# Delta-rule loop with a 128x4x64 state: carried, query and update products as alternating 64-wide tiles

## What is computed

```python
def gated_delta_rule_chunked(q, k, v, g, beta):
    """S_t = a_t (I - b_t k_t k_t^T) S_{t-1} + b_t k_t v_t^T, o_t = S_t^T q_t. Chunked WY form."""
...
    def step(state, inp):
        u_i, w_i, q_i, k_i, a_i, gl = inp
        v_new = u_i - jnp.einsum("bhid,bhde->bhie", w_i, state)
        o_i = jnp.einsum("bhid,bhde->bhie", q_i, state) + jnp.einsum("bhij,bhje->bhie", a_i, v_new)
        state = state * gl[..., None, None] + jnp.einsum("bhid,bhie->bhde", k_i, v_new)
        return state, o_i
```

## Time and profile before

| | |
|---|---|
| median of 3 runs | 2689.47 us (2685.22 to 2690.39) |
| span of the profiled execution | 2685.3 us |
| granted TensorE clock, mean of the span | 0.985 |
| TensorE busy | 2583.9 us, 96% |
| VectorE, ScalarE, GpSimd busy | 1817.1, 926.3, 549.2 us |

### The profile page before, as it was taken

One profiled execution on the slowest core, in us unless ns is written; L12 is line 12 of the kernel. 1 busy time (PEld: TensorE's weight loads), 2 busy tenths in 40 slices (PEclk: granted clock), 3 DMA queues, 4 the chain that ended last, 5 costly groups with the idle time before them and its releaser, 6 DMA issues. The chain is left out here.

```text
span 2685.3 us, 35832 instructions
## 1 busy us (share of the span) xinstructions
PE 2583.9 (96%) x14026; PEld 2060.8 (77%) x14026; DVE 1817.1 (68%) x2735; ACT 926.3 (34%) x1610; POOL 549.2 (20%) x265
## 2 busy tenths in 40 slices
PE   7999999999899999999999999999999999999998
PEld 5875558884478887788888888867997888887787
DVE  5894997772667668999773553333277666666987
ACT  4335454420444545333332222232233223232432
POOL 1212544430000004333201222134400000003330
PEclk9999999999999999999999999999999999999999
DMA  4011032230133336333221222243413222225231
GB/s 162 32 64 67 32 126 96 90 133 24 55 114 118 103 118 223 111 110 126 91 82 53 78 70 75 81 166 108 145 55 88 79 87 79 87 79 214 100 126 63
DMA packets 192759, 262.24 MB, mean 98 GB/s; under 512 B 15952, under 2 KB 121808, under 8 KB 192208
## 3 DMA queue, kind: packets, MB, share of 16 engines
q1 hardware_dynamic: 192592, 259.95, 28.6%
HBM read 196.80 MB, written 61.93 MB: 96 GB/s over the span
## 5 line engine op out<-in xcount | busy, mean ns | idle before, releaser
L1381 PE MATMUL ps<-gl_t,gl_slot 128*128 128x512 f32 x1056 | 244.6, 391 | 2.4 <-DVE gl_t L3986 2.4
L1389 PE MATMUL ps<-b_hi,a_hi 128*128 128x512 f32 x592 | 231.6, 391 | 9.5 <-DVE sb L3630 7.6
L1381 PEld LDWEIGHTS ps<-gl_t,gl_slot 128*128 128x128 f32 x1056 | 199.3, 189 | 44.6 <-DVE gl_t L3986 3.1
L2756 POOL TENSOR_TENSOR s_raw<-ff_raw 128x1024 f32<-128x1024 f32 x2 | 5.1, 2545 | 962.6 <-DMA ff_raw<-hid_rows 513.6
L3630 DVE TENSOR_TENSOR sb<-sb,ps 128x512 f32<-128x512 f32 x272 | 173.5, 680 | 33.3 <-PE ps L1389 33.2
L1381 PE MATMUL ps<-gl_b,gl_slot 128*128 128x512 f32 x768 | 182.1, 395 | 3.7 <-DVE gl_slot L4018 3.7
L1381 PE MATMUL ps<-ff_t,slot 128*128 128x512 f32 x768 | 179.2, 393 | 4.4 <-DVE ff_t L3284 4.4
L1381 PE MATMUL ps<-H_hi,tw_hi 128*128 128x512 f32 x448 | 175.6, 392 | 0.0
L1381 PE MATMUL ps<-H_rest,tw_hi 128*128 128x512 f32 x448 | 174.4, 389 | 0.0
L1381 PE MATMUL ps<-H_hi,tw_lo 128*128 128x512 f32 x448 | 174.3, 389 | 0.0
L1381 PEld LDWEIGHTS ps<-gl_b,gl_slot 128*128 128x128 f32 x768 | 146.4, 191 | 35.1 <-DVE gl_slot L4018 2.4
(11 more groups left out here) (475 smaller groups left out, 6053.9 us busy)
## 6 DMA issues: line engine op xcount, KB each, us to landing
wraw<-in_w_ff SPq DMA_DIRECT2D x16, 1024.0 KB, 5.9
ff_raw<-ff_rows SPq DMA_DIRECT2D x8, 2048.0 KB, 7.9
slab_raw<-in_w_ff SPq DMA_DIRECT2D x16, 1024.0 KB, 5.1
ff_rows<-quad SPq DMA_DIRECT2D x61, 256.0 KB, 2.0
traw<-in_w_in SPq DMA_DIRECT2D x28, 512.0 KB, 4.3
wq_raw<-in_w_in SPq DMA_DIRECT2D x6, 2048.0 KB, 8.5
wraw<-in_w_gate SPq DMA_DIRECT2D x22, 512.0 KB, 3.9
wraw<-in_w_up SPq DMA_DIRECT2D x22, 512.0 KB, 5.1
```

The lines of the kernel that those rows point to most:

```text
L1381: mm = nc.tensor.matmul(out_ap, stationary(a, k), moving(c, k), start=(k == 0 and n == 0), stop=(k == kts - 1 and n == 2))
L1389: mm = nc.tensor.matmul(out_ap, stationary(a, k), moving(c, k), start=(fresh and k == 0 and n == 0), stop=(k == 1 and n == 2), skip_group_ ...
L2756: G.tensor_tensor(s1, s3, a22, ALU.add).then_inc(dn_as, 1)
```

## The change

The state is kept compact, 128 partitions by 4 by 64: head 2q in the upper 64 partitions, head 2q+1 in the lower. Keys times state becomes, per direction, 8 products with 64 rows of contraction, 128 output rows and 64 columns, alternating between the two halves of the partitions and between two banks. The query-times-state products are made the same way and now stand as one group per direction ahead of that direction's scores-times-values products. The update becomes 8 products of 64 output rows and 64 columns per direction, alternating between the two halves of the output partitions. `forward` alternates between the directions product by product. The keys are decayed ahead of time on GpSimd (a new product of decay and keys into `KdT`, in `decayed_queries`), so VectorE's multiplication by the decay in `less_carried` goes away. The results of the heads of one parity lie in one bank and are taken away with a stride.

```diff
-            order += [("kS", i, d) for d in both] + behind(0, 1)
-            order += pair("y", 0) + behind(2) + pair("w", 1) + behind(3)
+            order += [("kS", i, d, x) for d in both for x in both] + behind(0, 1)
+            order += pair("y", 0) + behind(2, 3) + pair("w", 1)
...
-        Sbd = [[area(gd + 1024 * b + 512 * d, 4, P) for d in range(2)] for b in range(2)]
+        Sc = [[area(gd + 512 * b + 256 * d, 4, HD) for d in range(2)] for b in range(2)]
+        KdT = [area(gd + 1024 + 512 * d, 4, P) for d in range(2)]
...
                 for q in range(4):
-                    mm = nc.tensor.matmul(ps[:, b, q * P:(q + 1) * P], pair_tile(KTall, q, d, i), Sbd[d][i % 2][:, q, :],
-                                          start=True, stop=True)
+                    for x in both:
+                        mm = nc.tensor.matmul(ps[:, banks[x], q * HD:(q + 1) * HD], half(KdT[d], 2 * q + x),
+                                              half(Sc[d][i % 2], 2 * q + x), start=True, stop=True)
...
                 for h in range(HEADS):
+                    for d in both:
+                        rows = block_rows(d, s)
+                        mm = nc.tensor.matmul(ps[rows, banks[d], h * HD:(h + 1) * HD], Gm[i % 2][d][:, h, rows],
+                                              yv[i % 2][d][:, h * HD:(h + 1) * HD], start=True, stop=True)
+                        if h == HEADS - 1:
+                            mm.then_inc(full[banks[d]], 1)
...
+                    for x in both:
+                        cols = slice((2 * q + x) * HD, (2 * q + x + 1) * HD)
+                        mm = nc.tensor.matmul(ps[x * HD:(x + 1) * HD, b, q * HD:(q + 1) * HD], Kdec[d][:, cols],
+                                              yv[i % 2][d][:, cols], start=True, stop=True)
...
+            def carried_outputs(i, d):
...
+                pe.wait_ge(gdn_qd, 2 * i + d + 1)
+                for q in range(4):
+                    for x in both:
+                        nc.tensor.matmul(ps[:, banks[x], q * HD:(q + 1) * HD], half(QdT[(i + 2) % 3][d], 2 * q + x),
+                                         half(Sc[d][i % 2], 2 * q + x), start=(q == 0), stop=False, skip_group_check=True)
+
+            def own_outputs(i, d, x):
...
+                for q in range(4):
+                    h = 2 * q + x
+                    mm = nc.tensor.matmul(ps[:, b, q * HD:(q + 1) * HD], ATm[i % 2][d][:, h, :],
+                                          yv[i % 2][d][:, h * HD:(h + 1) * HD], start=(i == 0),
+                                          stop=(i == 0 or q == 3), skip_group_check=True)
+                mm.then_inc(full[b], 1)
...
+                else:
+                    carried_outputs(i - 1, 1)
+                    own_outputs(i - 1, 1, 0)
+                forward(i, 1)
+                if i > 0:
+                    own_outputs(i - 1, 1, 1)
...
+                    if i > 1:
+                        for x in both:
+                            wait_full(pool, G_GDN, GDN_AT[("kS", i - 1, d, x)])
+                    if i > 0:
+                        G.tensor_tensor(KdT[d], QdT[(i + 2) % 3][d], KTall[:, :, t * P:(t + 1) * P], ALU.mult
+                                        ).then_inc(gdn_keys, 1)
+                        pool.wait_ge(gdn_keys, 2 * (i - 1) + d + 1)
...
-                    V.tensor_tensor(heads_of(Xw[d], HD), heads_of(ps[:, b, :], HD),
-                                    args[:, ECUM, at:at + HEADS].unsqueeze(2).broadcast_to([P, HEADS, HD]), ALU.mult
-                                    ).then_inc(drained[b], 1)
-                for d in both:
-                    ready("kS", i, d)
-                    V.tensor_tensor(Xw[d], KVt[i % 2][d][:, GW:2 * GW], Xw[d], ALU.subtract).then_inc(gdn_X, 1)
+                    for x in both:
+                        b = arrived("kS", i, d, x)
+                        V.tensor_tensor(heads_of(Xw[d], HD)[:, x::2, :], heads_of(KVt[i % 2][d][:, GW:2 * GW], HD)[:, x::2, :],
+                                        heads_of(ps[:, b, 0:256], HD), ALU.subtract).then_inc(drained[b], 1)
...
-                V.tensor_tensor(Sbd[d][(i + 1) % 2], Sbd[d][i % 2],
-                                eglP[:, at, :].unsqueeze(2).broadcast_to([P, 4, P]), ALU.mult).then_inc(gdn_ss, 1)
+                V.tensor_tensor(Sc[d][(i + 1) % 2], Sc[d][i % 2],
+                                eglP[:, at, :].unsqueeze(2).broadcast_to([P, 4, HD]), ALU.mult).then_inc(gdn_ss, 1)
...
-            for d in both:
-                ins = V.memset(Sbd[d][1].rearrange("p a b -> p (a b)"), 0.0)
-            ins.then_inc(gdn_S0, 1)
```

More of the change, by code:

```diff
@@ L1006, in front, with rest_taken @@
             return 0, FRONT_AT[key]
+        def rest_taken(eng, i):
+            for d in range(2):
+                for x in range(2):
+                    wait_drained(eng, G_GDN, GDN_AT[("kS", i, d, x)])
         slab_last = [front("dense", 3, 1), front("dense", 7, 1), front("dense", 11, 1), front("SV", 7)]
@@ L1607, in solve, with forward @@
                             mm.then_inc(full[banks[d]], 1)
[L1609 to L1616, removed]
-                for h in range(HEADS):
-                    mm = nc.tensor.matmul(ps[rows, b, h * HD:(h + 1) * HD], Gm[i % 2][d][:, h, rows],
-                                          yv[i % 2][d][:, h * HD:(h + 1) * HD], start=True, stop=True)
-                mm.then_inc(full[b], 1)
+            def forward(i, s):
+                banks = []
+                for d in both:
+                    if s == 1:
+                        for x in both:
+                            ready("kk", i, d, x)
+                    ready("y", i, d, s - 1)
+                    banks.append(bank("w", i, d, s))
+                for h in range(HEADS):
+                    for d in both:
+                        rows = block_rows(d, s)
[3 more added lines that the diff above has]
+                            mm.then_inc(full[banks[d]], 1)
             def update(i, d):
@@ L1630, in update @@
                 mm.then_inc(full[b], 1)
[L1632 to L1649, removed]
+            def carried_outputs(i, d):
+                banks = [bank("o", i, 2 * d + x) for x in both]
+                if i == 0:
+                    return
+                pe.wait_ge(gdn_qd, 2 * i + d + 1)
[3 more added lines that the diff above has]
+                                         half(Sc[d][i % 2], 2 * q + x), start=(q == 0), stop=False, skip_group_check=True)
@@ new lines, in own_outputs @@
+            def own_outputs(i, d, x):
+                ready("y", i, d, 3)
+                ready("kq", i, d, x)
+                b = where(G_GDN, GDN_AT[("o", i, 2 * d + x)])[0]
+                for q in range(4):
[4 more added lines that the diff above has]
+                mm.then_inc(full[b], 1)
@@ L1673, in _ @@
                     scores("kk", i + 1, 0)
-                for d in both:
-                    forward(i, d, 2)
+                forward(i, 2)
                 if more:
@@ L1680, in _ @@
                     scores("kk", i + 1, 1)
-                for d in both:
-                    forward(i, d, 3)
+                forward(i, 3)
                 if more:
@@ L1688, in _ @@
                         update(i, d)
-            outputs(NT - 1, 0, 1, 2, 3)
+            for d in both:
+                carried_outputs(NT - 1, d)
+                for x in both:
+                    own_outputs(NT - 1, d, x)
             def mix_product(t, h, b, ks):
@@ L3089, in state_add @@
                         dve.wait_ge(gdn_ss, 2 * (i - 1) + d + 1)
-                    for x in both:
-                        part = slice(HD * x, HD * x + HD)
-                        dst = Sbd[d][(i + 1) % 2][part, :, part]
-                        new = heads_of(ps[part, b, :], P)[:, :, part]
-                        ins = V.tensor_tensor(dst, dst, new, ALU.add) if i > 0 else V.tensor_copy(dst, new)
+                    dst, new = Sc[d][(i + 1) % 2], heads_of(ps[:, b, 0:256], HD)
+                    ins = V.tensor_tensor(dst, dst, new, ALU.add) if i > 0 else V.tensor_copy(dst, new)
                     ins.then_inc(drained[b], 1)
@@ L3149, in _ @@
             dve.wait_ge(c_out, 32)
-            for d in both:
-                ins = V.memset(Sbd[d][1].rearrange("p a b -> p (a b)"), 0.0)
-            ins.then_inc(gdn_S0, 1)
-            dve.wait_ge(gdn_S0, 1)
             for t in range(1, NT, 2):
```

55 lines of the change are left out of this document (26 added, 29 removed).

## The result

The changed kernel takes 2722.77 us (median of 4 runs, 2719.57 to 2730.84) against 2688.44 us for the kernel before beside it (4 runs, 2685.22 to 2690.39). The ratio is 1.0132, with a 95% interval of 1.012 to 1.0145: some 34 to 35 us slower. The forecast was 2688.4, no change. In the profiles the span went from 2685.3 to 2729.0 us, and the mean granted TensorE clock from 0.985 to 0.964. The profiled execution of the changed kernel is the longest of its four (2730.84 us); the other three have a mean granted clock of 0.967 to 0.969 and are 7 to 11 us shorter, so the account that follows is for some 8 us more than the median.

What follows compares the result with a forecast made beforehand. TensorE bounds most of an iteration, VectorE's chain the two 5.25 us stretches. -2.4 - 6 x 0.5 + 5 x 0.6 + 0.3 + 1.0 = -1.1 us, giving 2688.4 us, no change; own range 2684 to 2694, stated range 2680 to 2702.

Steps and rivals of the forecast that it cites:

- Carried products cost the same at half the width: Keys times state in the head: twice as many products of half the width take 1.84 us against 1.89.
- Update 1.4, between 0.93 and 1.87: State update in column halves: 1.4 us against 2.07 before, the middle between two bounds.
- The head: Stretch from update to first solve, 6.68 us, set by TensorE; to gain 0.5 us, ends 0.8 and 0.0.
- Forward 1.0, and nothing won by it in the 5.25 us stretches: Interleaved forward takes 1.0 us, not 1.71; second to third and third to fourth solve gain 0, VectorE's subtraction starting later.
- First to second solve 6.3, for the lock: First state_decay meets GpSimd's running product, both reading SBUF: +0.6 us on 5.69, ends +0.3 and +0.9.
- GpSimd's lock costs more: Rival, chance 0.07: second state_decay delays the drain by 1.0 too, +0.9 at the first; +6.5 over the forecast, 2695.
- Iterations 0 and 1 gain 2.4: Start of the loop: first forward of iteration 1 starts 2.1 us earlier, 2.4 with shorter forward; ends 1.0 and 3.4.
- Last outputs +1.0: Final outputs, 9.67 us at half clock: about +1.0 for half-tile records and shape changes, ends 0.5 and 3.
- From span to time: Profile's span of 2684.2 us turned into a measured time by adding 4.2 us: 2688.4.
- column groups do not overlap: Rival, chance 0.07: forward stays 1.71 us, 1.8 us more an iteration over six; +12, 2701.
- the clock falls in the loop: Rival, chance 0.08: gaps of 1 us in the 5.25 us stretches halve TensorE's clock; +17, 2706.

Runs made afterwards that it cites:

- gaps filled: Changed kernel with 4 products of no use, 0.85 us, ahead of every second, third and fourth solve, written into a free bank and overwritten: 2688.34 us, ratio 0.9999.
- forward apart: Changed kernel with the forward products as before, eight of direction 0, then eight of direction 1: 2688.59 us, ratio 0.9985.
- the update whole: Changed kernel with the update as four full 128x128 products per direction as before, the state still compact: 2704.3 us, ratio 1.0044.
- spare products: Products whose results are overwritten, where TensorE idles; in the kernel before, added in iterations 0, 1 and 7: 2690.37 us, ratio 1.0003.

## Why the prediction was wrong

Its costing of a full-clock iteration held:

- *Carried products cost the same at half the width*: 1.83 us for a forecast 1.84.
- *Update 1.4, between 0.93 and 1.87*: 1.20. The head took 5.95 us, a gain of 0.73 for a forecast 0.5, inside the bounds.
- *Forward 1.0, and nothing won by it in the 5.25 us stretches*: 1.02, and 498.82 - 493.57 = 5.25. The chain through VectorE's weighting and subtraction is the bound there, with forward at 1.02 as at 1.71.
- *First to second solve 6.3, for the lock*: 6.23, with the decay at 1.01 us. The second `state_decay` (0.72 us) ended at 494.52, ahead of the drain at 494.70, so the rival *GpSimd's lock costs more* is out.
- *Iterations 0 and 1 gain 2.4*: 0.8. The forward product of iteration 1 started at 429.80 against 429.64, in a loop that began 2.3 us later: 2.1 us gained up to there, as forecast. But from there TensorE ran on at half clock until past 437 us (rows below), and output, solve and scores gave back most of the gain. This term was mis-sized by the clock too.
- *Last outputs +1.0*: 643.52 - 632.65 = 10.87 us for 9.67, +1.2, at half clock before and after.
- *From span to time*: the forecast put 4.2 us between them. Every run on record has its time 1.7 to 2.1 us above its span, so some 2 of the 4.2 were scatter of the profiled execution.
- The rival *column groups do not overlap* is out: forward, whose pairs share all rows, took 1.02 us for 1.71, and the update 1.20 for 32 records, where 32 records of forward one after the other took 1.71. The rule of the Trainium skill ("TensorE: Matmul & The Clock Gate", Part 3, "The mechanism") that a load overlaps a running matmul only in another row group, or by the background buffer, did not keep these pairs apart.

The stretch behind that forward product in iteration 1, columns as in the earlier trace rows, in the kernel before:

```profile
434.00:437.00 3.00, 3.00 (x71) 2.79 (x66) 2.63 (x5) 0.58 (x1) 0.45 (x1) 1.00 1.02 381
```

and in the changed kernel, at half clock and with 42 matmul records for 71:

```profile
434.00:437.00 3.00, 3.00 (x42) 2.83 (x40) 1.61 (x3) 0.58 (x1) 2.92 (x4) 0.50 0.93 337
```

The step that failed is the one under the sum: full clock in iterations 2 to 6. It stood as the rival *the clock falls in the loop*, with a chance of 0.08 and a price of 17 us. Both were too small. The price was worked out for two forward products an iteration; in fact the clock stayed down for 22 us at a time, over head, outputs, solves and scores, at 9.2 us an iteration, and for the whole last iteration, 12.7 more. I had read the sign that speaks for it: the earlier trace rows show 0.50 behind the wait of iteration 1, which was 2.65 us long, and 0.51 behind the waits of iteration 7, where only the scores are missing. The waits of iteration 7, 0.63 to 1.00 us, were no longer than the gaps that I forecast. TensorE timeline of the kernel before:

```profile
586.20 1.08 PE L1604 MATMUL ps<-sb 32*32 32x64 f32 x32 [0.99 <-DVE sb L3101]
...
590.69 1.08 PE L1604 MATMUL ps<-sb 32*32 32x64 f32 x32 [1.00 <-DVE sb L3101]
```

I took gaps of this size, more than one to an iteration, for harmless.

What the runs show in its place: the gaps bring the clock down, and with the shorter update products it stays down longer. With the gaps filled (2688), or with forward apart (2689), the clock holds in iterations 2 to 6 with every half tile in place. With two gaps of 1.2 us and none of the new products it falls and is back within some 4 us (2707); so it does with the changed kernel's gaps and the update whole (2704). With all of the change it stays down for 22 us (2723). Whether the half-tile carried and query products have a part in it is not shown: the two kernels without them that alternate forward (2693 each) also lack the largest gap. So my own accounting, "TensorE's shorter products cost nothing where TensorE isn't the bound", was right for the chain and wrong for the clock: work taken off an engine that waits was work that kept its clock up. Why the falls come at each second update and not at each, how much idle time it takes, and which property of a product brings the clock back, stays open; the runs only order the kernels.

## What to carry to other kernels

Where TensorE waits on another engine, making its products shorter wins nothing and can halve its clock for everything around; look at the granted clock by stretch before and after, and count the longer form as filler that may be worth keeping. If a shorter form is wanted elsewhere in the loop, pair it with work in the gaps: a few products into a bank that is free anyway, but only where the engine is idle, since at half clock or in a full stretch they are paid in full. And a VectorE product of two SBUF tiles belongs where GpSimd rests: 0.6 us of VectorE's time here, 0.4 us of an iteration.

## What the runs showed of the hardware beyond that

The granted clock stayed at 0.50 for 22 us in which TensorE's records had no gap at all: being busy by the records did not bring it back sooner. In the kernel with the whole update it was back after one such update, 3.55 us. Whole products alone do not settle it: the last outputs of the kernel before, 128x128 and 128x64 products of the full array without a gap, ran for 9.67 us and nearly all of it at half clock. The spare products have only 32 output rows and still held the clock up: in the kernel before at 1.00 through the last iteration, where it had fallen without them. Column pairs of 128*64 and 128*32 tiles with 64 columns take 37 and 32 ns a record (1.20 and 1.02 us for 32) where full contraction one after the other takes 53 ns; the 64*128 row pairs with 64 columns take 57 ns (1.83 us for 32).
